# Two-block transformer kernel: squares of the first norm added by VectorE, weight units raised between the input's blocks, gate rows made in three parts

## The reference

```python
def rmsnorm(x, gain):
    y = x * rsqrt(mean(x * x, axis=-1) + 1e-6)
    return y * gain

def token_mixer(xn, w_in, b_in, ...):          # xn = rmsnorm(x, norm_mix_pre)
    proj = xn @ w_in + b_in                    # 1024 -> 14 groups of 256, and 2 x 4 gate columns
    (m_q, m_k, m_v, m_o, m_i, m_f, c_b, c_c, c_h, a_q, a_k, a_v, h_q, h_f, h_i, h_g) = split(proj)
    h_m = mlstm_chunkwise(m_q, m_k, m_v, m_i, m_f)     # gates: cumsum(log_sigmoid(f)), running maximum
    y_c = c_b * causal_dwconv(c_c * c_h, sconv_w)
    y_a = moba_attention(a_q, a_k, a_v, rel_bias)
    o_h = hgrn2_chunkwise(silu(h_q), 1 - f_gate, log(f_gate), h_i)
    return concat(norm(h_m) * sigmoid(m_o), y_c, y_a, norm(o_h) * silu(h_g)) @ w_out
...
x = x + rmsnorm(token_mixer(...)); then cross attention, a gated FFN, and the whole second block
```

## Time and profile before

| | |
|---|---|
| median of 3 runs | 2359.19 us (2358.59 to 2364.32) |
| the profiled execution | 2358.33 us, of which the span of the trace is 2356.5 us |
| granted TensorE clock, mean | 0.973 of full speed |
| TensorE matmuls busy | 2213.4 us (94% of the span) |
| VectorE, ScalarE, GpSimd busy | 1049.4, 847.9, 814.7 us (45%, 36%, 35%) |

### The profile page before, as it was taken

The page is one execution under the profiler, slowest core; times in us unless marked ns, Lnnn a source line. Parts: engine busy times, 40 slices in busy tenths (PEclk is TensorE's granted clock), DMA queues, the critical chain, the costliest instruction groups (busy, mean ns, idle before and its releaser), DMA issues.

```text
span 2356.5 us, 27011 instructions
## 1 busy us (share of the span) xinstructions
PE 2213.4 (94%) x9984; PEld 1732.2 (74%) x9984; DVE 1049.4 (45%) x1542; ACT 847.9 (36%) x1256; POOL 814.7 (35%) x343
## 2 busy tenths in 40 slices
PE   6788989879999998898899999999999998999999
PEld 5676357658888885574678888878878876888887
DVE  3455474666552525437533212235652575322121
ACT  5332343442221233345543323343432433433231
POOL 2322013414444442120244444443334223444443
PEclk9899999989999999999999999999999999999999
DMA  3212012212332242110123222332222222222333
GB/s 137 71 54 72 28 45 99 72 36 89 123 109 98 97 136 89 45 63 10 51 93 97 93 97 98 99 105 72 72 65 88 72 63 63 96 92 98 98 98 99
DMA packets 54966, 193.35 MB, mean 82 GB/s; under 512 B 6096, under 2 KB 6352, under 8 KB 54480
## 3 DMA queue, kind: packets, MB, share of 16 engines
q1 hardware_dynamic: 50400, 181.58, 23.7%
q10 hardware_dynamic: 4464, 10.36, 1.3%
HBM read 189.82 MB, written 2.10 MB: 81 GB/s over the span
## 4 chain that ended last, share of the span: by engine, by line
PE 72%; issue 14%; DVE 9%; POOL 4%; ACT 2%; DMA 0%; POOLq 0%; SPq 0%; DVEq 0%; ACTq 0%
PE gemm_ps L493 21%; PE gemm_ps L494 21%; PE gemm_ps L495 21%; POOL wl L462 4%; PE out_ps L860 2%; DVE tmp L1571 1%; DVE arena L1925 1%; DVE tmp L1932 1%; PE turn_ps L688 1%; DVE arena L1571 1%; PE score_ps L679 1%; DVE x L1593 1%; PE out_ps L698 1%; DVE xl L1571 1%; PE score_ps L852 1%
## 5 line engine op out<-in xcount | busy, mean ns | idle before, releaser
L462 POOL TENSOR_TENSOR wl<-raw,wh 128x1024 fp32r<-128x1024 f32 x339 | 814.5, 2404 | 1523.8 <-ACT wh L1087 1523.8
L493 PE MATMUL gemm_ps<-xh,wh 128*128 128x512 f32 x1512 | 616.1, 407 | 54.9 <-DVE xl L1571 21.7
L1087 ACT ACTIVATE wh<-raw 128x1024 fp32r<-128x1024 f32 x339 | 358.8, 1059 | 776.1 <-DMA raw<-w_in 751.1
L494 PE MATMUL gemm_ps<-xl,wh 128*128 128x512 f32 x1512 | 593.8, 393 | 0.0
L495 PE MATMUL gemm_ps<-xh,wl 128*128 128x512 f32 x1512 | 593.5, 393 | 0.0
L494 PE MATMUL gemm_ps<-arena_r,wh 128*128 128x512 f32 (+1 forms) x1124 | 432.4, 385 | 0.0
L493 PEld LDWEIGHTS gemm_ps<-xh,wh 128*128 128x128 f32 x1512 | 287.3, 190 | 137.1 <-issue 58.3
L493 PE MATMUL gemm_ps<-arena_r,wh 128*128 128x512 f32 (+1 forms) x868 | 334.6, 385 | 11.2 <-DVE arena_r L1576 10.2
L494 PEld LDWEIGHTS gemm_ps<-xl,wh 128*128 128x128 f32 x1512 | 287.5, 190 | 67.3 <-issue 9.9
L495 PE MATMUL gemm_ps<-arena_r,wl 128*128 128x512 f32 (+1 forms) x868 | 332.5, 383 | 0.0
L495 PEld LDWEIGHTS gemm_ps<-xh,wl 128*128 128x128 f32 x1512 | 286.9, 190 | 61.1
(11 more groups left out here) (309 smaller groups left out, 2042.1 us busy)
## 6 DMA issues: line engine op xcount, KB each, us to landing
raw<-w_in SPq DMA_DIRECT2D x339, 512.0 KB, 3.3
arena<-na_in ACTq DMA_DIRECT2D x14, 256.0 KB, 2.7
x<-x_in SPq DMA_DIRECT2D x8, 256.0 KB, 7.1
out<-x ACTq DMA_DIRECT2D x8, 256.0 KB, 2.8
arena<-alibi_in ACTq DMA_DIRECT2D x6, 256.0 KB, 3.5
con<-con_in SPq DMA_DIRECT2D x1, 1432.0 KB, 12.7
arena<-moba_in ACTq DMA_DIRECT2D x1, 1024.0 KB, 4.9
arena<-mem_in ACTq DMA_DIRECT2D x1, 1024.0 KB, 4.8
```

Of the source, the lines that this page charges most:

```text
L462: pool.tensor_tensor(wl[:, k, :], raw[:, k, :], wh[:, k, :].bitcast(F32), ALU.subtract).then_inc(unit_split, 1)
L493: pe.matmul(o, wh[:, n % RING, w], h[:, kt, 0:width], start=(kt == 0), stop=False)
L494: pe.matmul(o, wh[:, n % RING, w], l[:, kt, 0:width], start=False, stop=False)
L1087: act.activation(wh[:, k % RING, :], raw[:, k % RING, :], ACT.Copy).then_inc(high_split, 1)
```

## The change

Four things are changed, all within the first 280 us:

1. The first norm's squares go the `added` way: `add_square(b)` on VectorE behind each `low`, and one `added_sum` on TensorE after unit 0, in place of eight `column_sum`.
2. ScalarE raises unit 0 before block 1, unit 1 before block 4 and unit 2 before block 6 of the input; unit 3 stays behind the root, and units 4 and 5 are raised before and within the gates' logarithms.
3. `gate_rows_made` is cut into `forget_sums`, `gate_rows_made` and `gate_limits`, with the emptying of units 5 and 6 between them; the clearing of the weight buffers moves behind the emptying of unit 8.
4. The gate columns are transposed and copied in `hgrn`, between units 9 and 10; of the four value blocks that `mlstm` turned at its beginning, the two of the attention are turned later: one in its last head, one after it.

```diff
@@ units (TensorE)
-                while first < 2:
+                while first < min(2, n0 + count):
@@ TensorE, mlstm
+            def turn_attended(b):
+                for t in range(T):
+                    m = pe.transpose(turn_ps[:, 0, t * P:(t + 1) * P], proj1[:, A_V + b, t * P:(t + 1) * P], ident)
+                m.then_inc(turned_v, 1)
             def mlstm():
-                take(gate_rows)
-                for t in range(T):
-                    m = pe.transpose(score_ps[:, 0, 4 * t:4 * t + 4], gate_b[0:4, t * P:(t + 1) * P], ident[0:4, 0:4])
-                m.then_inc(cols_turned, 1)
-                pe.wait_ge(bias_added, len(FIRST_BLOCKS) + 12)
-                turn_values([proj1[:, b, :] for b in (M_V, M_V + 1, A_V, A_V + 1)])
-                take(cols_ready)
+                pe.wait_ge(bias_added, len(FIRST_BLOCKS) + 6)
+                turn_values([proj1[:, M_V, :], proj1[:, M_V + 1, :]])
                 take(gate_rows)
...
                     for j in range(T + 2):
+                        if j == 1 and h == 3:
+                            turn_attended(0)
...
                 take(scores_used, 2)
+                take(copied_v)
+                turn_attended(1)
@@ TensorE, hgrn
                 turn_values([proj1[:, H_I, :], proj1[:, H_I + 1, :]])
+                take(gate_rows)
+                for t in range(T):
+                    m = pe.transpose(score_ps[:, 0, 4 * t:4 * t + 4], gate_b[0:4, t * P:(t + 1) * P], ident[0:4, 0:4])
+                m.then_inc(cols_turned, 1)
                 fill(FILL_START - 1)
+                take(cols_ready)
@@ TensorE, start
-            units(FIRST["in"], 1 + len(FIRST_BLOCKS), xh, xl, fresh=True, summing=True)
+            units(FIRST["in"], 1, xh, xl, fresh=True)
+            added_sum()
+            units(FIRST["in"] + 1, len(FIRST_BLOCKS), xh, xl)
@@ ScalarE, gate_logarithms
                 step(act.activation(gate_a[f, :], gate_a[f, :], ACT.Exp, scale=-1.0))
+                raise_to(5)
                 act.activation(gate_b[f, :], gate_a[f, :], ACT.Ln, bias=1.0).then_inc(gate_logs, 1)
@@ ScalarE, mlstm
-                take(cols_turned)
-                act.activation(small[:, 32:48], score_ps[:, 0, 0:16], ACT.Identity).then_inc(cols_ready, 1)
-                copy_values([v[:, :, b * P:(b + 1) * P] for v in (values1, values_moba) for b in range(2)])
+                copy_values([values1[:, :, b * P:(b + 1) * P] for b in range(2)])
...
+                    if h == 3:
+                        copy_attended(0)
...
                 m.then_inc(recurrence_copied, 1)
+                copy_attended(1)
@@ ScalarE, hgrn
                 copy_values([values1[:, :, b * P:(b + 1) * P] for b in range(2)])
+                take(cols_turned)
+                act.activation(small[:, 32:48], score_ps[:, 0, 0:16], ACT.Identity).then_inc(cols_ready, 1)
                 take(gate_arg)
@@ ScalarE, start
-                if b == 2:
-                    raise_to(0)
-            prepare(x, "norm_mix_pre", xh, loaded)
+                if b in (1, 4, 6):
+                    raise_to((1, 4, 6).index(b))
+            prepare(x, "norm_mix_pre", xh, loaded, added=True)
             raise_to(3)
             act.wait_ge(emptied, FIRST["in"] + 1)
+            raise_to(4)
@@ VectorE, hgrn
                 for n, o in first[2:4]:
                     scaled(n, o)
+                forget_sums()
+                scaled(*first[4])
                 gate_rows_made()
-                for w in weights:
-                    done(dve.memset(w, 0.0))
+                scaled(*first[5])
+                gate_limits()
                 reset = edge[:, 3, :]
...
-                for n, o in first[4:]:
+                for n, o in first[6:]:
                     scaled(n, o)
+                for w in weights:
+                    done(dve.memset(w, 0.0))
@@ VectorE, start
                 low(x, "norm_mix_pre", xh, xl, b)
+                add_square(b)
```

More of the change, by code:

```diff
@@ L1253, in gate_logarithms, with copy_attended @@
                 step(act.activation(gate_a[f, :], gate_a[f, :], ACT.Exp, scale=-1.0))
+                raise_to(5)
                 act.activation(gate_b[f, :], gate_a[f, :], ACT.Ln, bias=1.0).then_inc(gate_logs, 1)
+            def copy_attended(b):
+                take(turned_v)
+                act.activation(values_moba[:, :, b * P:(b + 1) * P],
+                               turn_ps[:, 0, :].rearrange("p (t c) -> p t c", c=P), ACT.Identity).then_inc(copied_v, 1)
             def mlstm():
-                take(cols_turned)
-                act.activation(small[:, 32:48], score_ps[:, 0, 0:16], ACT.Identity).then_inc(cols_ready, 1)
-                copy_values([v[:, :, b * P:(b + 1) * P] for v in (values1, values_moba) for b in range(2)])
+                copy_values([values1[:, :, b * P:(b + 1) * P] for b in range(2)])
                 take(gate_sums)
@@ L1749, in pair_attention, with forget_sums @@
                 take(probs_turned, 3)
-            def gate_rows_made():
-                f, r = slice(32, 36), slice(0, 4)
-                one = edge[:, 0, :]
+            def forget_sums():
+                f = slice(32, 36)
                 take(gate_logs)
@@ L1756, in gate_rows_made, with gate_limits @@
                 done(dve.tensor_tensor(gate_g[f, :], gate_g[f, :], gate_b[f, :], ALU.subtract))
-                done(dve.tensor_tensor_scan(gate_a[f, :], one[f, :], gate_g[f, :], 0.0,
+                done(dve.tensor_tensor_scan(gate_a[f, :], edge[f, 0, :], gate_g[f, :], 0.0,
                                             ALU.mult, ALU.add))
+            def gate_rows_made():
+                f, r = slice(32, 36), slice(0, 4)
                 done(dve.tensor_copy(gate_g[r, :], gate_a[f, :]))
                 done(dve.tensor_tensor(gate_b[r, :], gates[r, :], gate_g[r, :], ALU.subtract), gate_rows)
-                done(dve.tensor_tensor_scan(gate_a[r, :], one[r, :], gate_b[r, :], 0.0,
+                done(dve.tensor_tensor_scan(gate_a[r, :], edge[r, 0, :], gate_b[r, :], 0.0,
                                             ALU.mult, ALU.max))
+            def gate_limits():
+                r = slice(0, 4)
                 done(dve.tensor_tensor(gates[r, :], gate_g[r, :], gate_a[r, :], ALU.add), gate_sums)
```

## The result

The changed kernel took 2348.54 us (median of 5 runs, 2342.24 to 2349.82) against 2359.19: 10.7 us or 0.45% faster by the medians. The ratio worked out from all runs is 0.9945 with a 95% interval of 0.9929 to 0.9961, which is 13 us (9 to 17). Forecast were 2344 us and a range of 2337 to 2351. The profiled execution is one of the longer ones (2348.79 us, span 2346.7).

A forecast was written before the change was run, and what follows sets the result against it. It took TensorE, with matmuls busy 94% of the span, as the bound, so only its waits and lower clock could be won; 4.5 + 11.2 - 0.75 + 0.55 = 15.5 us gave 2344 us, range 2337 to 2351.

The forecast's parts named there:

- Prologue, 4.5 us: First norm and input units: the wait for `wl` before unit 1 goes and unit 1 ends at 36.8, 4.5 us earlier.
- Units 4 and 5 raised earlier, nothing: ScalarE's work on the input units: VectorE's later emptying of unit 3 stays covered by 1.2 us, so no effect.
- Gate rows, 11.2 us: Input units 5 to 7: the 8.6 us wait before unit 7 goes and unit 7 runs 2.6 us shorter, 11.2 gained.
- Gate columns, -0.75: In `hgrn`, before unit 11: ScalarE waits for small transposes and copies, a loss of 0.75 us, between 0 and 1.5.
- Value blocks, +0.55: `mlstm` to attention: start 1.4 us shorter, later transposes cost 0.3 and 0.55 us, a net gain of 0.55 us.
- "After 300 us every row should only be shifted": Sign in the changed profile: rows after 300 us, past all the edits, only move in time; no size given.
- the fourth rival: No effect: freed time is lost again where ScalarE and GpSimd serve units between `hgrn`'s levels, 2359 us; chance 0.04.
- the first two terms: The sum's terms for the prologue and the gate rows, gains of 4.5 and 11.2 us.
- the last pair: The sum's terms for gate columns and value blocks, a loss of 0.75 us and a gain of 0.55 us.

The follow-up runs named there:

- E1: The prologue's edit alone (squares added by VectorE, units raised earlier) on the kernel before: 2354.78 us against 2360.11.
- E7: The changed kernel with units 1 to 3 raised behind the last square, only unit 0 between the blocks: 2339.71 us.
- E9: The changed kernel with the eight column sums back on TensorE between the blocks, the units' early raising kept: 2344.57 us.
- E2: The gate rows' three parts alone on the kernel before: 2347.50 us, ratio 0.9952.
- E3: Gate columns turned in `hgrn` and the attention's value blocks turned later, alone on the kernel before: 2362.73 us, ratio 1.0013.
- E5: The changed kernel with ScalarE putting the bias of unit 24 ahead of raising unit 27 at the attention's first item: 2341.76 us.
- E12: The changed kernel with the diffs of E5, E7 and E8 and unit 9 emptied early: 2327.16 us, ratio 0.9865.
- each mend: Single edits of the changed kernel: unit 27 raised later, unit 9 emptied early, units 1 to 3 raised behind the last square: 2341.76, 2337.74, 2339.71 us.
- E4: The changed kernel run again, unchanged: 2342.94 us (2342.36 to 2348.6, 6 runs), ratio 0.9931 to the kernel before.
- E8: The changed kernel with sixteen unread products of constants on TensorE in `hgrn`'s waits, ten between its halves: 2341.45 us.
- E11: The changed kernel with the diffs of E5 and E7 and unit 9 emptied early: 2334.13 us, ratio 0.9883.

## Why the prediction was right

The direction, the two large mechanisms and the range held. 2344 lies 4.5 us below the first median and 0.8 us above the median of all eleven runs. How near it came is partly luck: the times lie at 2342 to 2343 or at 2348 to 2350, three of the first five fell into the upper group, and nothing in the forecast knew of the groups. Point by point:

- *Prologue, 4.5 us.* Right in mechanism and nearly in size: 5.3 us alone (E1), 6.4 us until unit 1 is emptied in the changed kernel. The layout had the last `low` end at 26.8 (it was 26.6) and the `low` of blocks 4 and 5 lengthened by GpSimd (2.34 and 2.73 us), in the places named. What was too dark was the clock: it rose before the sums in the changed kernel's trace, so they took 1.7 us and not 3.3. That it could have gone the other way is seen in E1's profile, where it stayed low until 29.5 us and unit 1 was emptied at 36.1, near the forecast's 36.8. The rule of the Trainium skill (SBUF — State Buffer, "Who interferes with whom"), that the two engines' instructions exclude each other, was worth its place: with it the layout met the trace, and E7 priced two such meetings at 3.2 us. The step didn't ask which half of the edit pays; by E9 it is the earlier raising.
- *Units 4 and 5 raised earlier, nothing.* Right: no wait appears between units 2 and 9.
- *Gate rows, 11.2 us.* Right: from unit 1 to the transposes behind unit 9 the changed trace gains 11.0 us, and E2 gives 12.6 with an interval of 8.0 to 14.4.
- *Gate columns, -0.75.* The direct cost is right, 0.7 us until unit 11 begins (17.4 to 16.7 in the ledger); E3's trace has 0.7 us there too. Not foreseen was that unit 11 then took 1.3 us more at a later rise of the clock.
- *Value blocks, +0.55.* This is the term that failed. The shorter start of `mlstm` came (1.4 us), as did the transposes' cost (0.6 us twice), but the later transposes shift TensorE by 0.6 us against ScalarE, and with it VectorE behind GpSimd's next `wl`: 2.57 instead of 0.61 us. The whole fourth edit costs 2.6 us (0.9 to 5.2; E3) where the step had 0.2. I had called ScalarE's side idle time and had not asked what the shift does to which of VectorE and GpSimd comes first.
- *"After 300 us every row should only be shifted"*: not quite. Measured by GpSimd's rows, the shift wanders between -7.3 and -13 us (the latter near 1000 us) and ends at -9.8.
- *The clock between `hgrn`'s halves.* No step spoke of it. It accounts for most of what the profiled run gave back (5.0 us); that it makes the two groups is not shown. In the fourth rival I had named time lost again between the levels, at 0.04, but by service of the units and not by the clock.

The sum of the parts alone is 5.3 + 12.6 - 2.6 = 15.3 us, the forecast's sum 15.5. Two errors cancel in it: the first two terms were 2.2 us too small, the last pair 2.4 us too kind. Against the first median (10.7 us) the forecast's sum is 45% too large; against the median of all eleven runs (16.0 us) it is right, and it lies in the first interval (9 to 17 us).

What stays open: why the clock falls in that passage in some executions of the same kernel and not in others, and what makes the two groups, since no execution of the lower group was profiled and near relatives at 2341.55 to 2344.49 us had 0.82 in the passage like the upper group's second profile. Nor was the changed kernel run on the chips of E5 to E12, so each mend's size of 0 to 4 us hangs on a comparison across chips.

## What to carry to other kernels

Removing a gap in front of TensorE paid twice here, for the gap and for the unit behind it, which had run partly at half the clock (7.1 to 8.4 us instead of 5.4); and a stretch of small waits later on gave 5 us of it back, so look at the granted clock of every stretch after the edit and not only of the edited one. Where two engines exclude each other, ask of each shifted instruction which of the two now comes first: 0.2 us decided 2 us. When a wait disappears, ask what the next one is made of; here an engine that stood idle for 4.8 us held the buffer that TensorE wanted next, and one moved line was worth more than half of the prologue's edit.

## What the runs showed of the hardware

- One kernel, run again on one chip, has two groups of times 5 to 6 us apart (E4), and in its eleven runs they go with the mean granted clock (0.975 to 0.976 against 0.972 to 0.974). Ten useless products of 0.43 us, put into four waits of 1.0 to 1.6 us, held the clock at 1.00 over 28 to 32 us where it had been 0.70 to 0.82 (E8, and 0.74 in E11 against E12), and the stretch took 6 us less.
- Each of VectorE's operations that met a `wl` stood behind that one: with two `wl` in a row (5.11 us) two small operations that take 0.61 us alone took 4.67 us, 2.3 each, where beside a single `wl` they took 2.58 together. A `low` that met one ended about 0.55 us behind it in each of four rows (20.09 against 19.54 us, for one). In E7 a head start of 0.15 us was enough for VectorE to come first.
